# Five stage changes of a hybrid encoder step: the same instructions in another order

## The reference, cut to what matters

```python
h      = rmsnorm(x, norm1_w) * (1 + scale1) + shift1
u      = h @ w_in                       # pool_in | z | xBC | dt | gate_a | gate_b
a_out  = pool_mixer(u.pool_in) * pool_scale
xbc    = silu(dw(u.xBC) + conv_b)
y      = ssd(xbc, softplus(u.dt + dt_bias)) + d_skip * xs
b_out  = grouped_rmsnorm(y * silu(u.z)) # 4 groups of 512 channels
merged = sigmoid(gate_a) * (a_out @ w_branch_a) + sigmoid(gate_b) * (b_out @ w_branch_b)
x      = x + gate1 * (merged @ w_out)
h2     = rmsnorm(x, norm2_w) * (1 + scale2) + shift2
x      = x + gate2 * ((silu(h2 @ w_ffn_gate) * (h2 @ w_ffn_up)) @ w_ffn_down)
out    = rmsnorm(x, final_norm_w)       # and the new pool, conv and ssm states
```

## Time and profile before

| | |
|---|---|
| three runs | 2493.07, 2498.18, 2500.6 us; median 2498.18 us |
| span of the profiled execution | 2492.5 us |
| PE, matmul records | 2334.4 us, 94% of the span |
| PE, weight loads | 2252.1 us, 90% |
| DVE, ACT, POOL busy | 1269.8, 623.7, 104.9 us |
| HBM traffic | 103 GB/s over the span |

### The profile page before, as it was taken

One profiled execution on the slowest core, in us unless ns is written; L12 is line 12 of the kernel. 1 busy time (PEld: TensorE's weight loads), 2 busy tenths in 40 slices (PEclk: granted clock), 3 DMA queues, 4 the chain that ended last, 5 costly groups with the idle time before them and its releaser, 6 DMA issues.

```text
span 2492.5 us, 36698 instructions
## 1 busy us (share of the span) xinstructions
PE 2334.4 (94%) x13811; PEld 2252.1 (90%) x13811; DVE 1269.8 (51%) x2056; ACT 623.7 (25%) x1007; POOL 104.9 (4%) x151
## 2 busy tenths in 40 slices
PE   5699999998899999998999897989999999999995
PEld 5599999998799999988999896879999999999995
DVE  6665544555566767635557545543334434333345
ACT  1423223432333232322121423221111111111111
POOL 0000000000111111101000000010000000000000
PEclk9699999999899999988999998999999999999997
DMA  6265523332555465642223333211111111111104
GB/s 192 71 192 161 169 65 89 89 97 83 176 180 178 157 191 179 199 133 86 87 87 120 108 132 127 85 55 48 42 42 42 42 50 42 42 42 44 48 25 152
DMA packets 319867, 258.75 MB, mean 104 GB/s; under 512 B 13443, under 2 KB 293701, under 8 KB 319807
## 3 DMA queue, kind: packets, MB, share of 16 engines
q1 hardware_dynamic: 263535, 204.11, 27.1%
q10 hardware_dynamic: 52368, 41.57, 5.3%
q0 software_dynamic: 3904, 12.26, 1.4%
HBM read 195.69 MB, written 62.21 MB: 103 GB/s over the span
## 4 chain that ended last, share of the span: by engine, by line
PE 50%; issue 43%; DVE 4%; ACT 1%; DMA 1%; POOL 1%; SPq 0%; ACTq 0%; DVEq 0%; POOLq 0%
PE PS L988 28%; PE PS L1144 11%; PE PS L1126 2%; PE PS L1194 2%; PE PS L1120 1%; PE PS L1123 1%; DVE ada_sum L1382 1%; DVE hf L1400 1%; PE PS L1110 1%; PE PS L1133 1%; PE PS L1029 1%; PE PS L1067 1%; DMA ada_first<-in_w_ada 0%; PE PS L1205 0%; DVE pool_s L1653 0%
## 5 line engine op out<-in xcount | busy, mean ns | idle before, releaser
L988 PE MATMUL PS<-act_a_hi,w_hi 128*128 128x364 f32 (+1 forms) x1344 | 448.4, 334 | 25.2 <-DVE act_a_lo L1613 15.1
L1340 DVE TENSOR_TENSOR w_lo<-w_raw,w_hi 128x1024 fp32r<-128x1024 f32 x156 | 195.5, 1253 | 493.8 <-ACT w_hi L641 492.1
L988 PE MATMUL PS<-act_a_lo,w_hi 128*128 128x364 f32 (+1 forms) x1344 | 445.4, 331 | 0.0
L988 PE MATMUL PS<-act_a_hi,w_lo 128*128 128x364 f32 (+1 forms) x1344 | 445.2, 331 | 0.0
L1286 PE MATMUL PS<-act_b_lo,w_hi 128*128 128x364 f32 (+1 forms) x1056 | 347.7, 329 | 0.0
L1286 PE MATMUL PS<-act_b_hi,w_hi 128*128 128x364 f32 (+1 forms) x1056 | 347.5, 329 | 0.0
L1286 PE MATMUL PS<-act_b_hi,w_lo 128*128 128x364 f32 (+1 forms) x1056 | 347.5, 329 | 0.0
L641 ACT ACTIVATE w_hi<-w_raw 128x1024 fp32r<-128x1024 f32 x156 | 164.7, 1056 | 488.0 <-PE PS L988 213.0
L988 PEld LDWEIGHTS PS<-act_a_hi,w_hi 128*128 128x128 f32 x1344 | 256.2, 191 | 27.8 <-DVE act_a_lo L1613 16.4
L988 PEld LDWEIGHTS PS<-act_a_lo,w_hi 128*128 128x128 f32 x1344 | 256.1, 191 | 0.0
L988 PEld LDWEIGHTS PS<-act_a_hi,w_lo 128*128 128x128 f32 x1344 | 255.9, 190 | 0.0
(11 more groups left out here) (249 smaller groups left out, 3442.2 us busy)
## 6 DMA issues: line engine op xcount, KB each, us to landing
w_raw<-in_w_in SPq DMA_DIRECT2D x64, 512.0 KB, 5.2
acs_in<-acs_c SPq DMA_DIRECT2D x36, 512.0 KB, 5.4
ada<-in_w_ada SPq DMA_DIRECT2D x16, 1024.0 KB, 7.4
gp_s<-gp ACTq DMA_DIRECT2D x24, 544.0 KB, 3.4
w_raw<-in_w_ffn_gate SPq DMA_DIRECT2D x22, 512.0 KB, 3.8
w_raw<-in_w_ffn_up SPq DMA_DIRECT2D x22, 512.0 KB, 3.8
w_raw<-in_w_ffn_down SPq DMA_DIRECT2D x22, 512.0 KB, 3.6
xs_in<-xs_c SPq DMA_DIRECT2D x36, 256.0 KB, 3.0
```

Of the source, the lines that this page charges most:

```text
L988: e = pe.matmul(PS[:, n, 0:w], wt[a], at_[b][:, o:o + w], start=(k == 0 and q == 0), stop=(k == len(steps) - 1 and q == 2))
L1340: dve.tensor_tensor(w_split[v][1][:, :], w_raw[v][:, :], w_split[v][0][:, :].bitcast(F32), ALU.subtract)\
```

## The change

Five places, no instruction of work more or less. On ACT the increment that gives the first three xBC banks free moves ahead of the dt tables. On DVE the low part of the fourth slice moves from piece 7 to piece 6 of a group. On DVE in `merge_tile` the product of the `acc` row with its gate comes first, ahead of the three thirds. On PE tiles 0 and 1 of the output product are done together, one k step of each in turn, and each k waits for its own w_out low part. On PE the transposes of tile 8 move behind the first two thirds of the first FFN unit; that unit waits for the banks of the output product (`mm_free["out"]`) in place of `mm_free["ffn"]`.

```diff
+            act.sem_inc(mm_free["xbc"], 3)
+
             act.wait_ge(dt_vec, DV_TAB)
             act.activation(eacs_tab[:, :, :], dt_s[:, :, :], ACT.Exp).then_inc(dt_act, 1)
...
-            act.sem_inc(mm_free["xbc"], 3)
...
-            def out_tile(t):
+            def out_step(t, k):
                 L = CH if t < NCH - 1 else DEC
+                for a, b in PASSES:
+                    for h in range(2):
+                        e = pe.matmul(PS[0:L, 2 * (t % 2) + h, :], act_b[b][:, k, t * CH:t * CH + L],
+                                      wo_res[k // 4][a][:, k % 4, h * 512:(h + 1) * 512],
+                                      start=(k == 0 and a == b == 0), stop=(k == KT - 1 and a == 1))
+                return e
+
+            for k in range(KT):
+                pe.wait_ge(mg_lo, k + 1)
+                pe.wait_ge(lo_ready, U_OUT + k + 1)
+                for t in range(2):
+                    e = out_step(t, k)
+                    if k == KT - 1:
+                        e.then_inc(mm["out"], 1)
+            for t in range(1, NCH):
                 if t >= 2:
                     pe.wait_ge(mm_free["out"], t - 1)
-                for k in range(KT):
-                    if t == 0:
-                        pe.wait_ge(mg_lo, k + 1)
-                        if k % 4 == 0:
-                            pe.wait_ge(lo_ready, U_OUT + k + 4)
...
-                e.then_inc(mm["out"], 1)
-
-            out_tile(0)
-            for t in range(1, NCH):
-                out_tile(t)
+                    for k in range(KT):
+                        e = out_step(t, k)
+                    e.then_inc(mm["out"], 1)
                 turn(n2, xn[(t - 1) % 2][:, :, :], t - 1, 4 + 2 * ((t - 1) % 2), CH)
-            turn(n2, xn[0][:, :, :], NCH - 1, 4, DEC)
...
             def first_gate(n):
+                if n == 2:
+                    turn(n2, xn[0][:, :, :], NCH - 1, 4, DEC)
                 pe.wait_ge(n2.lo, 3 * n + 3)
-                pe.wait_ge(mm_free["ffn"], n + 1)
+                pe.wait_ge(mm_free["out"], NCH)
...
-                        if g < GROUPS - 1 and piece > 3:
+                        if g < GROUPS - 1 and 3 < piece < 7:
                             y_low(g + 1, piece - 4)
+                        if g < GROUPS - 1 and piece == 6:
+                            y_low(g + 1, 3)
...
                 dve.wait_ge(mg_vec, m * 5 + 5)
+                row = acc[:, ds(m, 1), :].rearrange("p o t -> p (o t)")
+                dve.scalar_tensor_tensor(gates[v][1][:, :], gates[v][1][:, :], 1.0, row, ALU.add, ALU.mult)\
+                   .then_inc(mg_vec, 4)
                 for n, (o, w) in enumerate(SUBS):
...
-                row = acc[:, ds(m, 1), :].rearrange("p o t -> p (o t)")
-                dve.scalar_tensor_tensor(gates[v][1][:, :], gates[v][1][:, :], 1.0, row, ALU.add, ALU.mult)\
-                   .then_inc(mg_vec, 4)
```

## The result

| | before | after |
|---|---|---|
| time, median (range), us | 2496.26 (2493.07 to 2500.6), 4 runs | 2474.63 (2470.69 to 2478.14), 4 runs |
| ratio, 95% interval | | 0.9911 [0.9896, 0.9927] |
| profiled execution, span, us | 2492.5 | 2476.4 (its time: 2478.14) |

The changed kernel is 21.6 us faster by the medians (18.2 to 26.0 by the interval); 2476.4 was forecast. The profiled execution is the slowest of the four. The one before was about 2 us faster than its median, if its time lies as far above its span as here (2478.14 against 2476.4). So the spans differ by only 16.1. For the single parts I therefore take the distance between the same two events in either trace; what one execution loses elsewhere stays out of that. Lines of the code have moved by one to seven (L988 is now L989, L1053 L1054, L1268 L1262, L1286 L1289).

The account below looks back on a forecast made before the run. The prediction took TensorE's (PE's) matmul stream plus its pauses as the bound. Gains of 7.1, 5.9, 6.6 and 2.2 us summed to 21.8, taking the median of 2498.2 to 2476.4 us, range 2467 to 2486.

Parts of the forecast that it names:

- Part 1: Convolution columns: PE starts at once after the dt products, 5.27 us of pause and 1.8 of clock fall saved, 7.1.
- Part 2: Three group changes: the pauses for the fourth slice's low part go, 1.98 us each, 5.9 together.
- The cover fits with nothing over: Group changes: DVE's y_low(2) lasts to about 1192.7, just covering ACT's high copy, which ends at 1192.69.
- Part 3: Merge: row product first lets tile 7's low parts start about 1.2 us earlier; lower end 0.
- Part 4: First output tiles: 10.05 us wait vanishes, a 4.9 us pause with 1.8 clock fall comes; gain 6.6 us.
- Part 5: First FFN gate: two thirds fill the pause, 3.6 us pause and 1.8 clock fall before the third; gain 2.2 us.
- The sum: Whole kernel: 7.1 + 5.9 + 6.6 + 2.2 = 21.8 us less, from median 2498.2 to 2476.4.
- (a): Rival: the clock doesn't fall in one or both new pauses, 3.6 us more gained, 2472.8; chance 0.12.
- (b): Rival: output stage gives nothing because x rows or norm chain land late, 2483.0; chance 0.12.
- (c): Rival: the pair of output tiles runs at half clock, 17.8 of 21.8 gone, 2494.2, no change; chance 0.04.
- (d): Rival: the low clock lasts into the tiles after the pair, slower, all seven 2563; chance 0.02.
- (e): Rival: the merge order saves nothing at tile 7, price 1.2 us; no chance of its own given.

Follow-up runs that it names:

- both orders: Changed kernel with output tile 2 ahead of tile 0's transposes and tile 8's transposes ahead of the second gate third: 2465.84 us, ratio 0.9872 to before.
- part1_alone: Kernel before with only the increment of the convolution's three banks moved ahead of ACT's wait for the dt tables: 2488.66 us, ratio 0.9973.
- the kernel with the long pause: Changed kernel with PE made to wait before the convolution columns until DVE's copy of acs_row is made: 2486.58 us, one run.

## Why the prediction was right, point by point

**Part 1** was right in all its terms: 7.0 of 7.1, the clock stayed up, and the second unit's weights did not come late.

**Part 2** was right in mechanism and 0.4 low. I had counted 1.98 from start to start and left out the slower first matmul (0.44 against 0.33). "The cover fits with nothing over" held: no bank sum came late. Not in the sum was a fall of the clock in the old pauses: it came behind two of their twelve in the four traces that have them and cost 1.5 us each time (last section), and it is gone with the pauses.

**Part 3** is the step that held only in part: "its sum, the first two w_out low parts and with them the loads of the next two come 1.3 earlier, and DVE reaches tile 7 1.3 earlier". The first half holds. DVE does not reach tile 7 by as much earlier, since it still waits for the fourth row's load. On average 0.6 was left of 1.2. I had named 0 as the lower end, and the sum took the upper.

**Part 4** was right in its order of events: no wait within the pair, one pause of 5.0 us (4.9 forecast) before the transposes, a fall of the clock in it. The first transposes came 7.2 us earlier than in the one trace before, where 8.4 was forecast; by the means of the four and the five traces they came 8.6 earlier. Mis-sized was the price of the fall: 1.8, taken over from the earlier trace rows. From the first transposes to the second it took 14.36 us instead of 11.80, so this fall cost 2.6; in the five traces it is 2.6 to 2.9. In the earlier trace rows PE worked at 0.50 for 3.8 us, here for 5.4 (1539.73 to 1545.1), and in both about half of that is lost. By the means 5.8 was gained of 6.6, and the fall's price is all of the difference; part 3's shortfall is made up by the old order, which took longer in the other three traces than in the one I had read.

**Part 5** is the same: the pause of 3.59 against 3.6 forecast, and the third third, 6.40 us long (1638.90 to 1645.30) instead of 4.0, paid 2.4 for the clock where I had 1.8. In the seven traces with this pause it paid 1.6 to 2.6.

**The sum.** The gain was forecast as 21.8; the medians say 21.6, the traces 20.9 with the means above and 19.7 without them. All lie within the measurement's interval of 18.2 to 26.0. The time itself was 1.8 too high because I started from the median of three runs, 2498.18, where that of four is 2496.26. That the gain was hit to 0.2 is luck: the falls were counted too cheap and part 3 too high, each by more than that, and the measurement doesn't resolve 0.2.

**The rivals.** (a), no fall in the new pauses, is out by the stretches shown; seven traces have the pause before the first transposes and seven the one before the third third, and the clock fell at all fourteen. (b) was touched and not reached: the x rows were 0.18 us late. (c) and (d) did not come: the pair ran at 1.00 from 1514 on, and not even slowed low parts kept it down. The rule of the Trainium skill (TensorE: Matmul & The Clock Gate, section "A second HAM failure mode: psum-queue depth-cycling"), on which (c) leaned, speaks of frequent small pauses between groups; no run here had them in the pair (with the slowed low parts there was one of 0.34 us and one of 3.14). (e) was about half of the truth on part 3.

## What to carry to other kernels

A pause on the bounding engine is best filled with the next piece of work that waits for nothing new, and after each such move the question is which piece is now first in its queue without cover: here the pair of tiles took away the cover of the first transposes, and putting the next tile ahead of them won 5.5 us more by the medians. Take the price of a clock fall, and the length of the stretch that a change replaces, from several executions and not from one: the fall before the first transposes cost 1.6 to 2.9 us in seven traces, and the old output stage took 123.3 to 125.5 us in four. And a gain that reaches the bound only through a load is worth what the load's landing shows, not what its issue shows.

## What the runs showed of the hardware

Whether the clock falls is not settled by the length of the one pause before it. At 2.17 us it stayed up, at 3.41 it fell eight matmuls after PE had taken up work again. With tile 8 put early it fell behind a pause of only 1.68 (1.69 with both orders), which had a pause of 0.53 (1.21) and transposes of 128 columns some 5 us ahead and transposes of 64 columns behind it. Which of these counted, no run here separates.

Nor does the same pause with the same work around it end the same way each time. In part1_alone the clock fell behind the 1.82 us of the first group change, and that group took 66.26 us to the next change instead of 64.73:

```profile
1192.31 0.44 PE L989 MATMUL PS<-act_a_hi,w_hi 128*128 128x364 f32 x1 [1.82 <-DVE act_a_lo L1614]
...
1193.00:1196.00 3.00, 3.00 (x12) 3.00 (x11) 0.47 (x2) 2.64 (x3) 0.00 (x0) 0.50 0.43 131
```

In the trace of the kernel before it did not, at the same place:

```profile
1198.00:1200.00 2.00, 2.00 (x14) 2.00 (x13) 0.78 (x2) 2.00 (x3) 0.00 (x0) 1.00 0.09 25
```

Counted over all thirteen traces, a fall came behind 2 of the 12 pauses of 1.82 at group changes, behind 3 of 13 pauses of 2.3 for a bank sum (acc), and at 8 of 13 pauses of 2.79 in the pooling branch. It came at all 14 of the pauses that the change makes (3.6 and 4.9 to 5.7). So the length of the pause alone does not decide, and the one execution with 2.17 shows that the clock can stay up there, not that it does.

The group sums, 288 matmuls of one column, took 42.9 us in the changed kernel, 44.8 before and 47.0 in the kernel with the long pause, with the same work; in the thirteen traces they took 41.2 to 47.2. In the kernel with the long pause the last matmul of branch A comes 8.2 us later than in the changed one: 3.5 less 0.9 for an earlier start and 1.5 are the pause's and the clock's, and 4.1 are this row's. So this row alone moves by 6 us where the runs of the kernel before spread over 7.5, and a single run does not resolve 5 us of this kernel.

```profile
L1195 PE MATMUL PS<-ones,ysq 128*128 128x1 f32 (+1 forms) x288 | 42.9, 285 | 0.0
```

```profile
L1196 PE MATMUL PS<-ones,ysq 128*128 128x1 f32 (+1 forms) x288 | 47.0, 299 | 0.0
```
